# Dilated attention inside the odd projection's units, in a new order of units, with pooling beside them

## The reference, cut to what matters

```python
mod = silu(c) @ ada_w[l] + ada_b[l]          # 6 x 1024 values
sh1, sc1, g1, sh2, sc2, g2 = split(mod, 6)
h = rmsnorm(x, norm_mix_g[l]) * (1 + sc1) + sh1
z = h @ odd_w_in                             # 1024 -> 5120
q, k, v = split(z[..., :4608], 3)            # 3 dilation groups x 8 heads x 64
# per head: scores of three groups (window 128/512/2048, dilation 1/4/16) with ALiBi,
# softmax per group, groups combined by their denominators
o_c = dilated_attention(q, k, v, slopes)     # 512 wide
o_d = multiscale_pool(z[..., 4608:])         # window means 2,4,8,16 minus u, then 128x128 each, scale
x = x + g1 * (concat(o_c, o_d) @ odd_w_out)
h = rmsnorm(x, norm_ffn_g[l]) * (1 + sc2) + sh2
gate, val = split(h @ ffn_w_up[l], 2)        # 2 x 2816
x = x + g2 * ((silu(conv3(gate)) * val) @ ffn_w_down[l])
out = rmsnorm(x)
```

## Time and profile before

| | |
|---|---|
| median of three runs | 879.2 us (875.46 to 880.14) |
| span of the profiled execution, first to last instruction | 868.7 us; no separate device time is given for it |
| TensorE busy | 797.4 us, 92% |
| VectorE, ScalarE, GpSimd busy | 599.5, 422.8, 71.7 us |
| odd projection | 457.3 to 572.2 us |
| dilated attention | 572.2 to 634.2 us |
| pooling matmuls, second modulation sum | 634.2 to 641.7 us |
| output projection | 641.7 to 666.1 us |

### The profile page before, as it was taken

The page is one execution under the profiler, slowest core; times in us unless marked ns, Lnnn a source line. Parts: engine busy times, 40 slices in busy tenths (PEclk is TensorE's granted clock), DMA queues, the critical chain, the costliest instruction groups (busy, mean ns, idle before and its releaser), DMA issues.

```text
span 868.7 us, 17243 instructions
## 1 busy us (share of the span) xinstructions
PE 797.4 (92%) x6580; PEld 750.3 (86%) x6580; DVE 599.5 (69%) x870; ACT 422.8 (49%) x664; POOL 71.7 (8%) x89
## 2 busy tenths in 40 slices
PE   3399998986898999999989999999998999999996
PEld 2299996675788999999979899977787999999995
DVE  3876687779759999874466766667735777776444
ACT  4244464331246666663345444634344666666332
POOL 0200117000200000000020100050000000000000
PEclk9699998577899999999999999995579999999998
DMA  9999885322364999755563898852505576765511
GB/s 360 332 261 330 295 287 194 98 73 81 116 175 122 289 289 290 221 198 207 185 224 134 296 308 296 279 170 76 144 3 146 144 194 193 193 194 194 193 49 48
DMA packets 160047, 171.17 MB, mean 197 GB/s; under 512 B 5178, under 2 KB 142339, under 8 KB 158979
## 3 DMA queue, kind: packets, MB, share of 16 engines
q1 hardware_dynamic: 151363, 139.11, 51.0%
q0 software_dynamic: 8640, 31.46, 10.2%
HBM read 169.50 MB, written 1.05 MB: 196 GB/s over the span
## 4 chain that ended last, share of the span: by engine, by line
PE 79%; DVE 12%; DMA 5%; issue 2%; ACT 1%; SPq 1%; POOLq 0%; DVEq 0%; ACTq 0%
PE acc L1049 50%; PE big L1049 14%; DMA ada_raw<-in_ada_w 4%; PE aux L1178 2%; DVE mod_acc L774 2%; DVE mod_acc L714 2%; DVE qk L287 2%; PE big L1318 2%; PE aux L1101 1%; PE big L1201 1%; PE acc L1206 1%; PE acc L1330 1%; DVE w_lo L704 1%; PE big L1323 1%; PE acc L1112 1%
## 5 line engine op out<-in xcount | busy, mean ns | idle before, releaser
L1049 PE MATMUL acc<-h_hi,w_hi 128*128 128x256 f32 x1248 | 351.4, 282 | 17.3 <-DVE h_lo L754 14.8
L1049 PE MATMUL acc<-h_lo,w_hi 128*128 128x256 f32 x1248 | 348.6, 279 | 0.0
L1049 PE MATMUL acc<-h_hi,w_lo 128*128 128x256 f32 x1248 | 348.6, 279 | 0.0
L704 DVE TENSOR_TENSOR w_lo<-w_raw,w_hi 128x1024 fp32r<-128x1024 f32 x220 | 263.1, 1221 | 105.0 <-ACT w_hi L474 104.9
L474 ACT ACTIVATE w_hi<-w_raw 128x1024 fp32r<-128x1024 f32 x220 | 224.5, 1050 | 101.3 <-PE big L1049 62.4
L1049 PEld LDWEIGHTS acc<-h_hi,w_hi 128*128 128x128 f32 x1248 | 238.4, 191 | 19.6 <-issue 17.7
L1049 PEld LDWEIGHTS acc<-h_lo,w_hi 128*128 128x128 f32 x1248 | 238.1, 191 | 0.4
L1049 PEld LDWEIGHTS acc<-h_hi,w_lo 128*128 128x128 f32 x1248 | 237.8, 191 | 0.0
L714 DVE SCALAR_TENSOR_TENSOR mod_acc<-ada_raw,cact,mod_acc 128x1024 f32<-128x1024 f32 x80 | 106.8, 1338 | 21.8 <-DMA ada_raw<-in_ada_w 21.6
L1049 PE MATMUL big<-hid_hi,w_hi 128*128 (+1 forms) x352 | 97.2, 276 | 0.0
L1049 PE MATMUL big<-hid_lo,w_hi 128*128 (+1 forms) x352 | 97.2, 276 | 0.0
(11 more groups left out here) (184 smaller groups left out, 911.8 us busy)
## 6 DMA issues: line engine op xcount, KB each, us to landing
w_raw<-in_ffn_w_up SPq DMA_DIRECT2D x88, 512.0 KB, 5.0
ada_raw<-in_ada_w POOLq DMA_DIRECT2D x60, 512.0 KB, 5.6
w_raw<-in_ffn_w_down SPq DMA_DIRECT2D x44, 512.0 KB, 4.0
w_raw<-in_odd_w_in SPq DMA_DIRECT2D x40, 512.0 KB, 5.0
w_raw<-in_even_w_in SPq DMA_DIRECT2D x32, 512.0 KB, 6.0
ada_raw<-in_ada_w SPq DMA_DIRECT2D x20, 512.0 KB, 3.8
ada_first<-in_ada_w SPq DMA_DIRECT2D x5, 1024.0 KB, 8.1
w_raw<-in_even_w_out SPq DMA_DIRECT2D x8, 512.0 KB, 5.2
```

The costliest lines, as they stand in the source:

```text
L704: dve.tensor_tensor(w_lo[:, n % SPLIT, part], w_raw[:, n % RAW, part], w_hi[:, n % SPLIT, part].bitcast(F32), ALU.subtract).then_inc(s_lo, 1)
L1049: ins = pe.matmul(dst, lhsT, rhs, start=start and n == 0, stop=stop and n == 2, skip_group_check=True)
```

## The change

- The units of the odd projection come in the order of `ODD`: queries and keys of every second unit (heads 0 to 3), the values of those heads, the two pooling units, then the rest.
- Steps 0 to 10 of the attention stand inside units: one step inside each of the positions 9 to 16 and 18, two inside position 19 (`BESIDE`). On TensorE a step comes after 8 of a unit's 16 groups of three matmuls (after 5 and 10 where there are two); on VectorE and ScalarE it comes ahead of that position's eviction and splits. The remaining steps follow, with halves of two output units between them.
- Scores use two banks (`big` 0 and 1), values `big` 2; the negation is folded into the reduction.
- Pooling on GpSimd starts after position 10, its matmuls stand inside position 17.
- All modulation tiles of this phase are loaded by SP: 24 among the loads of the odd layer, each placed six positions after the tile whose buffer it takes was used, and added one or two per position. The last 8 (for g2) are loaded among the units of `ffn_w_down` of layer 1 and added there; their sum stands ahead of the down unit 9.
- `w_used`, `s_lo` and the four raw buffers are as before.

```diff
+ODD = (0, 2, 4, 6, 8, 10, 12, 14, 16, 18, 19, 1, 3, 5, 7, 9, 11, 13, 15, 17)
+FIRST_HEADS, POOL_UNITS, LAST_SCORES = 9, 11, 17
+BESIDE = {9: (0,), 10: (1,), 11: (2,), 12: (3,), 13: (4,), 14: (5,), 15: (6,), 16: (7,), 18: (8,), 19: (9, 10)}
+BESIDE_ENDS = 11
+LATE_TILES = (1, 2, 1, 2, 1, 2, 1, 2, 1, 1, 1, 1, 1, 1, 1, 1, 1, 1, 1, 1)
+LAST_TILES = (0, 1, 1, 1, 1, 1, 1, 1, 1, 0, 0)
...
@@ SP
+            def late_tile(j):
+                k, q = (j // 3, j % 3) if j < 24 else (j - 24, 3)
+                sp.wait_ge(ada_used, ADA3 + j - 1)
+                sp.dma_start(ada_raw[:, j % 2, :], ada_w[1, k * P:(k + 1) * P, 2048 + q * 1024:3072 + q * 1024]).then_inc(
+                    late_landed[j % 2], 16)
+            used_after = [p for p, count in enumerate(LATE_TILES) for _ in range(count)]
+            j = 0
+            for p in range(N_OI + N_OO):
...
+                while j < 24 and (j < 2 or used_after[j - 2] + 6 <= p):
+                    late_tile(j)
+                    j += 1
...
             up(1, UP1)
-            down(1, DN1)
+            j = 24
+            for u in range(N_DN):
+                load(0, DN1 + u, ffn_w_down[1].rearrange("(u k p) n -> u p k n", p=P, k=2)[u])
+                for _ in range(LAST_TILES[u]):
+                    late_tile(j)
+                    j += 1
@@ GpSimd
-            with pool.Fori(0, KT) as k:
-                for q in (0, 1):
-                    tile_in(1, k, 2048 + q * 1024, q, k, ADA3 // 2)
...
-            pool.wait_ge(z_evicted, N_EI + N_OI)
+            pool.wait_ge(z_evicted, N_EI + POOL_UNITS)
@@ ScalarE
+            for p in range(N_OI):
+                for s in BESIDE.get(p, ()):
+                    dilated(s)
+                if p == LAST_SCORES:
+                    act.wait_ge(pool_mixed, 1)
...
+                odd_step(p)
...
+            nc.scalar.activation(h_hi[:, 4:8, :], work[:, 4:8, :], ACT.Copy).then_inc(h_hi_ready, 1)
+            for s in range(BESIDE_ENDS, STEPS + 7):
+                dilated(s)
@@ VectorE, down projection of layer 1
+                    j = 24
+                    for u in range(N_DN):
+                        if u < N_DN - SPLIT:
+                            split_lo(0, first_down + u + SPLIT)
+                        for _ in range(LAST_TILES[u]):
+                            late_tile(j)
+                            j += 1
+                    keep_mods(4, 8, aux[:, 1])
+                    take_mods(4, 1, 40, 8, aux[:, 1])
@@ VectorE, odd projection
+            def dilated(s):
+                base, r = STEPS, s - 4
+                if 0 <= r < STEPS:
+                    j = r // 2
+                    dve.wait_ge(exp_done, base + r + 1)
+                    link(dve.reciprocal(stat[:, r % 4, 3:4], stat[:, r % 4, 2:3]))
+                    dve.wait_ge(attended, base + r + 1)
...
+                                      stat[:, r % 4, 3:4], None, ALU.mult).then_inc(out_taken, 1)
+                if s < STEPS:
+                    dve.wait_ge(scored, base + s + 1)
...
+                    link(dil_shift(s))
+                    dve.tensor_reduce(stat[:, s % 4, 1:2], cs[s % 4], AX_X, ALU.max, negate=True).then_inc(shifted, 1)
+            for p in range(N_OI):
+                for s in BESIDE.get(p, ()):
+                    dilated(s)
+                split_lo(0, OI + p + SPLIT)
+                for _ in range(LATE_TILES[p]):
+                    late_tile(j)
+                    j += 1
+            mixed_lo(MIX_AT[1] + 1, slice(4, 8))
+            for s in range(BESIDE_ENDS, STEPS + 4):
+                dilated(s)
@@ TensorE
+                r = s - 3
+                if 0 <= r < STEPS:
...
+                    pe.wait_ge(probs_kept, base + r + 1)
+                    if r >= 1:
+                        pe.wait_ge(out_taken, base + r)
+                    dil_values(big[:, 2, r % 2 * DH:(r % 2 + 1) * DH], cpt[:, r % 2, :], 2 * (r // 4) + r % 2,
+                               r // 2 % 2).then_inc(attended, 1)
...
+            dilated(11)
+            pe.wait_ge(z_evicted, N_EI + N_OI)
+            half_of(0, (4, 5, 6, 7), pooled, True)
+            dilated(12)
+            dilated(13)
+            half_of(1, (4, 5, 6, 7), pooled, True)
+            for s in range(14, STEPS + 2):
+                dilated(s)
+            pe.wait_ge(shifted, 2 * STEPS)
+            mod_sum(3, ADA4, 24, big[:, 1])
+            for s in range(STEPS + 2, STEPS + 6):
+                dilated(s)
+            mod_turn(3, 24, big[:, 1])
+            half_of(0, (0, 1, 2, 3), attended_at, False)
+            half_of(1, (0, 1, 2, 3), attended_at, False)
...
@@ TensorE, down projection
+                if l == 1:
+                    mod_sum(4, ADAS, 8, aux[:, 1], 24)
+                down_unit(0, first_down + N_DN - 2)
```

More of the change, by code:

```diff
@@ L1 @@
 from contextlib import ExitStack
+from functools import partial
 import numpy as np
@@ L756, in norm, with mixed_lo @@
                                              op1=ALU.subtract).then_inc(h_lo_ready, 1)
-            def mixed_lo(value, half):
-                part = slice(4 * half, 4 * half + 4)
+            def mixed_lo(value, part):
                 dve.wait_ge(h_hi_ready, value)
@@ L994, in _ @@
                                                       a.rearrange("p (b r) -> p b r", r=RES)))
-            dve.wait_ge(acc_zeroed, 3)
-            def late_step(first, tile0, per):
-                def step(i, n):
-                    if not (isinstance(i, int) and n + SPLIT in (OO, OO + 1)):
-                        split_lo(i, n + SPLIT)
-                    for tile in range(tile0 + per * (n - first), tile0 + per * (n - first + 1)):
-                        add_tile(i * 2 * per + tile % 16 // 2, 2 * (tile // 16) + tile % 2, tile % 2, i * 2 * per,
-                                 (ADA3 + tile) // 2)
-                return step
@@ L1067, in feature_major, with token_major @@
                                 count >= len(steps) - 2 if h_from is not None else k == KT - 1)
+                    if count + 1 in BREAKS[len(beside)]:
+                        beside[BREAKS[len(beside)].index(count + 1)]()
                 ins.then_inc(w_used, 1)
-            def token_major(n, a, order=None):
+            def token_major(n, a, order=None, beside=()):
                 for t in range(TT):
@@ L1077, in token_major @@
                                     hk, k == 0, k == KT - 1, swap=True)
+                        count = t * KT + k + 1
+                        if count in BREAKS[len(beside)]:
+                            beside[BREAKS[len(beside)].index(count)]()
                 ins.then_inc(w_used, 1)
@@ new lines, in pool_mix, with beside_unit @@
+            def pool_mix():
+                pe.wait_ge(s_odd, 32)
+                pe.wait_ge(pool_step, POOL_STEPS)
+                pe.wait_ge(shifted, STEPS + 8)
+                for g in range(4):
+                    ins = pe.matmul(big[:, g // 2, (g % 2) * T:(g % 2 + 1) * T], poolw[:, g, :], pmean[:, g, :], start=True,
+                                    stop=True)
+                ins.then_inc(pool_mixed, 1)
+            def beside_unit(p):
+                if p == LAST_SCORES:
+                    return (pool_mix,)
+                return tuple(partial(dilated, s) for s in BESIDE.get(p, ()))
@@ new lines, in _ @@
+            for p, u in enumerate(ODD):
+                n = OI + p
+                split_ready(0, 2, n)
+                if p >= 2:
+                    pe.wait_ge(z_evicted, N_EI + p - 1)
+                if 12 <= u < 16:
+                    token_major(n, p % 2, beside=beside_unit(p))
+                elif 16 <= u < 18:
+                    pe.wait_ge(wrapped, 4)
+                    token_major(n, p % 2, staggered, beside=beside_unit(p))
+                else:
+                    feature_major(n, p % 2, NORM_AT[2] if p == 0 else None, beside=beside_unit(p))
@@ new lines, in half_of @@
+            def half_of(u, ks, ready, first):
+                n = OO + u
+                split_ready(0, 2, n)
+                for count, k in enumerate(ks):
+                    if k % 2 == 0:
+                        pe.wait_ge(h_lo_ready, ready[k // 2])
+                    for g in (0, 1):
+                        cols = slice(k * 256 + g * P, k * 256 + (g + 1) * P)
+                        ins = three(acc[:, u, g * T:(g + 1) * T], (w_hi[:, n % SPLIT, cols], w_lo[:, n % SPLIT, cols]),
+                                    (h_hi[:, k, :], h_lo[:, k, :]), first and count == 0 and g == 0,
+                                    not first and count == len(ks) - 1)
+                if not first:
+                    ins.then_inc(w_used, 1)
@@ L1363, in _ @@
+            for s in range(STEPS + 2, STEPS + 6):
[3 more added lines that the diff above has]
+            half_of(1, (0, 1, 2, 3), attended_at, False)
+            norm_sum_of(3, 0, 2)
+            for u in (2, 3):
+                units(OO, OO + u, 1, feature_major, x_updated, 16)
+                norm_sum_of(3, 2 * u - 2, 2 * u)
```

257 lines of the change are left out of this document (138 added, 119 removed).

## The result

The changed kernel takes **934.97 us** (median; 929.29 to 940.9) where the kernel before, run beside it, takes 878.62 (875.46 to 880.14): ratio 1.0661, 95% interval 1.0605 to 1.0716. The sign was forecast and the size was not: 56.3 us slower instead of 32.8. In all that follows, medians and ranges hold every execution of a kernel, and the ratios leave out the single slow ones, 1.5% or more above its fastest.

What follows compares the result with a forecast made beforehand. TensorE, busy for 92% of the span, was taken as the bound, partly at low clock. Middle -3.3, down projection ring +34.4 and clock +1.7 give +32.8 us on 868.7: span 901.5, median 912, range 894 to 928.

Steps and rivals of the forecast that it cites:

- The ring: Layer 1 down projection: loads queue behind tile waits on SP, 10.4 us per round where a unit takes 5.45; +34.4 us.
- Tile 31 and the picks: Down projection, ahead of unit 9: TensorE waits 4.8 us for the last tile, then eight picks take 1.8; 6.6 together.
- Rivals 1 and 3: 1: clock low through the down projection, +8, 920, chance 0.12; 3: no ring forms there, 884 or 872, chance 0.08.
- Positions 0 to 8: First units of the odd projection: spread tiles win back half of 3.9 us lost to late landings; -2.0 us.
- Positions 9 to 19: Odd projection units with steps inside: 97.1 us, 82.8 of it work and 14.3 waits for VectorE.
- rival 4: Odd projection: the clock falls despite steps inside units, step prices of 2.2 become 3.8; +15, 927; chance 0.06.
- GpSimd beside VectorE: Pooling in the odd projection lengthens VectorE's splits and tiles: 1 us, left inside the rounding; by the skill's rule up to 6.
- The late tile: Odd projection, positions 0 to 8: half of the 3.9 us lost to late-landing tiles was taken as gone.
- After the projection: Remaining attention steps, output units and sums: 55.6 us, with a wait near 6 at step 11 and 24 picks at 5.4.
- Rival 2: Odd stretch runs at TensorE's pace, values' wait does not bind: gain 31.5 instead of 3.3, 884 us; chance 0.08.

Runs made afterwards that it cites:

- x1: The changed kernel with SP issuing each layer-1 down-projection modulation tile six units after the one whose buffer it takes; 900.81 us, 1.0229 of the kernel before.
- x2: x1 with the last eight tiles added one position earlier, at down units 0 to 7; 898.44 us, 1.0189 of the kernel before.
- x3: x2 with VectorE taking the tokens of step s-3 behind step s's shift, instead of s-4's ahead of it; 869.4 us, 0.986 of the kernel before.
- y5: x2 with TensorE's values and token transposes placed after 14 of a unit's 16 groups instead of 8; 880.34 us, 1.0047 of the kernel before.
- x4: x2 with GpSimd's ten pooling instructions replaced by small memsets, pooling left out of the result; 895.46 us, 1.0111 of the kernel before.
- y3: x3 with ScalarE evicting and splitting ahead of the step's exp in positions with a step; 868.78 us, 0.9919 of the kernel before.
- y2: x3 with all attention steps taken out of the units and placed behind the projection; 886.46 us, 1.0106 of the kernel before.

## Why the prediction was right or wrong, by its steps

**The ring: right in mechanism, the stage 4.9 us too small.** The term that was mis-sized is the round, 10.4 us against 11.2. Tile 31 was used 74.6 us after the end of unit 1, where the working had 70.5; the last two units at the slower pace of the last section (5.85 and 5.66 us instead of 5.45) add 0.6. The round came from the landing: 5.6 with the issue, where the chain has 0.33 and 0.43 of issue and then 5.40 to 5.76 until the second half has landed, 6.2 to 6.6 in all. I took a tile of 0.5 MB ahead of two halves at the stretch's full 420 GB/s; these are at or over my upper bound of 6.2. 36.1 of the 41.0 us stood in the terms, and x1 shows 32.1 of them as SP's order.

**Tile 31 and the picks: right.** 4.7 measured for the wait against 4.8 (x1), and 4.3 returned when the tiles come earlier (x2).

**Rivals 1 and 3 fell.** The clock in the ring is 0.85 on average, not low throughout, and the eight picks behind 8.0 us of waiting took 3.25 us (906.72 to 909.97 in the chain) where 1.8 and 1.7 for the clock were forecast. The ring formed. The Trainium skill (TensorE: Matmul & The Clock Gate, section "HAM oscillation — how this bites in real kernels") lets every burst behind a DMA wait begin throttled. Here, of the five units behind stops of 2.9 to 5.6 us, three began at the low level, one fell to it after 1 us, and the one at 846.5 us, behind a stop of 3.10, ran at 1.00 throughout. The low level cost nothing in the round, which waits for the landing.

**Positions 0 to 8: right** (-1.7 against -2.0).

**Positions 9 to 19: the failed step.** "From then on both loops lock ... 0.75 values, 2.72 the second half: 9.0 us per unit" took TensorE at full clock on both sides of a wait that the same sentence worked out. The waits were right: TensorE waited 14.1 us for the tokens where the sum has 14.3, first 5.01 (forecast 5.1), then 1.4 to 1.5 in positions 14, 15, 16 and 18 (the loop has 1.4) and 3.31 in position 19. What I had put at nothing is the clock behind them. I had given it a price after the projection and in the down projection, and put rival 4 (the clock falls inside the units) at 0.06, on the ground that 15 us of thin work had kept it. Here it fell in four of the six positions with such a stop: the second half took 5.14 us in position 13 and 4.41 in position 14, and 2.75 in position 15. By the intervals, positions 13, 14, 16 and 19 hold 10.8 of the 18.9 us; TensorE worked for some 18.6 us at the low level there, half of which, 9.3 us, is what the clock cost (an estimate from the narrow windows of the trace). That the granted clock follows the waits is shown by x3 and y5, which take the waits away in two ways and get 0.98 and 0.95 instead of 0.88. Why it fell behind some of the stops of 1.4 to 1.5 us and not behind others stays open; in x2 it fell behind two of 1.40 us and not behind one of 1.51. How the 23.9 us of x3 divide between wait and clock is read from its windows (13.0 and 10.7), not tried apart.

**GpSimd beside VectorE: mis-sized.** I put a term of 1 us "inside the rounding"; rows show 3.7 us of longer instructions and x4 returns 3.7. The single row of before (2.05 instead of 1.28) came from the end of a pooling instruction, and the overlap there was partial. The other estimate that the prediction gives beside it, up to some 6 us, was hardly nearer.

**The late tile: missed, 4.0 us.** I had taken half of the stall of before as gone; it came in position 9's interval instead, where two tiles landed 1.39 and 2.65 us late behind the loads, and which took 11.99 us instead of 8.0. y3 has a landing late by 2.25 there and takes 6.96: with the eviction ahead of the exp the late tile is off the path.

**After the projection: 2.9 too small**, 1.6 of it the sum of 24 picks, 7.0 instead of 5.4 us. I priced it at full clock; the trace has it at the low level from 660.3 to 663.6 us, which is the 1.6. It is the failed step once more: the clock fell behind a stop of only 1.0 us and 2.4 us of values, turns and transposes. The wait at step 11 was 6.20, forecast near 6.

**Rival 2** (TensorE's pace in the odd stretch) was false for this kernel, but it is what x3 and y3 make of it: 7.44 to 7.9 us in positions 13 to 16, and in y3 the middle 14.6 us under before, of the 31.5 that I had as its bound.

**Outside the sum:** 4.1 us ahead of the odd layer and 4.5 in the up projection of the profiled execution lie in identical code. They fit into the 11.4 us by which the two profiled executions stand apart from their medians (8.2 and 3.2, first section). Without them the terms miss by 26.4 us of the span: 21.5 in the middle, 4.9 in the down projection.

## What to carry to other kernels

A queue that issues DMAs in order is only as far ahead as its earliest wait: a transfer with a near wait placed ahead of one with a far wait turns four buffers into one; moving the issue back cost nothing here (x1). When small work is put between the halves of a long one, ask on every engine what stands behind it: the eviction that frees the next unit goes first, and a result that the long engine needs is taken before it asks. And where a sum has a wait on TensorE, even one of 1.5 us between dense halves, the work behind it is priced at both clock levels.

## What the runs showed that I had not expected

At a granted clock of 1.00 the same units run at two paces. The windows 740 to 760 us, inside the up projection of layer 1, of after and then of x1, have TensorE busy for all of the 20 us, with 172 and 179 matmuls:

```profile
740.00:760.00 20.00, 20.00 (x172) 20.00 (x171) 13.33 (x21) 12.64 (x19) 0.00 (x0) 1.00 0.60 170
```
```profile
740.00:760.00 20.00, 20.00 (x179) 20.00 (x178) 14.09 (x22) 13.34 (x20) 0.00 (x0) 1.00 0.65 181
```

A unit takes 5.65 or 5.44 us, a matmul 117.8 or 113.3 ns. The up projection of layer 0 has the short pace in before, after and x1 to x4 and the long one in y2 to y5; that of layer 1 has the long one in after, x2, x3 and y2. Kernels with identical code there differ by 4.5 us per up projection, so it is not the code of that stage. In layer 0 the two paces go with the two groups of runs, in layer 1 both occur within each group; the cause is open. Differences of stages under 5 us between two profiles can't be read without looking at this pace.
